# Gate and up of a SwiGLU layer: two of eight pairs of row tiles with seven block products for eight, on one Trainium2 core

## The chip, the cores and the metric

The kernel runs on one core of one Trainium2 chip. The metric is the device time of one execution in microseconds (us). The kernel before takes 2149.98 us, the median of three runs (2149.72 to 2150.53). Engines are named as in the profile: PE (TensorE matmul), PEld (TensorE weight load), DVE (VectorE), ACT (ScalarE), POOL (GpSimd), SP (SyncE, which issues most DMAs).

## What is computed

A decoder trunk of two layers over 256 rows of 2048 columns in float32. Each layer is an attention part and a SwiGLU channel mixer; the change touches only the mixer.

```python
def swiglu(h, w_gate, w_up, w_down):
    return (jax.nn.silu(h @ w_gate) * (h @ w_up)) @ w_down
...
        h = rmsnorm(x, ffn_norm[i])
        x = x + swiglu(h, ffn_w_gate[i], ffn_w_up[i], ffn_w_down[i])
```

`h` is 256 x 2048, `w_gate` and `w_up` are 2048 x 5632, `w_down` is 5632 x 2048. RMSNorm's division is applied after the product (`rstd`), its gains before it.

## The kernel before

**Split products.** A float32 product is made of three fp32r matmuls: high times high, high times low, low times high (`three`, L1490). A "half" is the unit of work of all engines: 128 x 1024 numbers of a weight. ACT rounds them to `w_hi` (`split`, L957), DVE subtracts to get `w_lo` (L1185), and PE uses both in 12 matmuls of 128 x 512 (`half`, L1496). The rows of x, transposed and split, lie ready in `xT_hi` and `xT_lo`, 16 tiles of 128 features by 256 rows.

**Queues and rings.** `walk` (L396) writes one order of work, and each engine walks it and issues its own part, strictly in that order. Weights arrive by SP's DMAs in chunks of 1 MB, two halves each, into the ring `raw` of four. `w_hi` and `w_lo` are rings of four halves (SPLIT = 4). In the place of half n ACT splits half n+3, which waits until PE has finished half n-1; DVE makes the low part of half n+2; PE multiplies half n when its low part is there (`lo_ready`).

**Gate and up.** The 5632 columns are 11 column blocks of 512 (FB = 11). For each, `ff_block` (L580) does a `block` of eight halves for gate into `acc[0:2]`, `gate` (silu by ACT, L1141), a `block` of eight for up into `acc[2:4]`, and `up` (product by DVE into `hid`, L1429). A loop runs it over nine column blocks.

**Hidden values.** They are transposed beside the next gate block, by `hidden` (L570): `hidden_words` (DVE, two copies into 16-bit words, L1441) in the place of half 1, `hidden_turn` (ACT issues four DMA transposes, L1152) in that of half 3, and the copy back into `hT` (DVE, L1451) in that of half 7. `hidden_turn` stands in ACT's own queue, between two splits:

```python
                act.wait_ge(words_ready, n.hT.value(1))
                act.nop(nofuse=True)
                for w in range(2):
                    for m in range(MT):
                        act.dma_start_transpose(wordsT[:, w, :, m * P:(m + 1) * P],
                                                words[:, w, m, :]).then_inc(wordsT_loaded, 16)
```

The down product (`rows`, L596) follows, with the first of its rows beside the last hidden block; its eight sums lie in all eight banks of PSUM (`down_bank`).

Of the kernel before, what the change touches and what calls it, by code (L numbers as in the profile page):

```python
# [22 lines left out]
P = 128  # L23
HD = 64
GROUP = 8
NB = 512
# [7 lines left out]
S384 = 3 * P  # L34

# [33 lines left out]
class Counts:  # L69


    def __init__(self):
        self.half = Count()
        self.chunk = Count()
        self.x = Count()
# [12 lines left out]
    @contextmanager  # L88
    def loop(self, eng, rounds, sets=(0, 0), **per):

        known = {"half": self.half, "chunk": self.chunk, "norm": self.norm, "qkT": self.qkT, "pair": self.pair,
                 "hT": self.hT, "kt": self.kt}
        every = [(v, per.get(k, 0)) for k, v in known.items()] + list(zip(self.sets, sets))
        start = [v.c for v, _ in every]
        with eng.Fori(0, rounds) as i:
            for v, k in every:
                v.i, v.per = (i, k) if k else (None, 0)
            yield i
            for (v, k), c in zip(every, start):
                assert v.c == c + k, (v.c, c, k)  # L100
                v.i, v.c, v.per = None, c + rounds * k, 0
# [87 lines left out]
def decoder_kernel(nc, widths, x_in, attn_norm, ffn_norm, even_w_in, even_q_norm, even_k_norm, even_sinks,  # L189
# [23 lines left out]
    HALVES = 4 + 8 * 8 + 2 * 4 * 8 + 3 * CG * 8 + 2 * (2 * FB * 8 + FK * 2)  # L213
    BQ = AQ + 2 * AK

    with ExitStack() as ctx:
# [13 lines left out]
        x = sb("x", [P, MT, D], F32)  # L230
        with ExitStack() as s1:
# [6 lines left out]
            wordsT = sb("wordsT", [P, 2, 4, SEQ], U16, s1)  # L238
        oT_hi = sb("oT_hi", [P, KT, SEQ], F32R)
# [40 lines left out]
        acc = [ctx.enter_context(nc.psum_tensor(f"acc{i}", [P, NB], F32)) for i in range(4)]  # L280
# [3 lines left out]
        down_bank = [work[0:2], acc[0:2], work[2:4], acc[2:4]]  # L284

        raw_loaded = [sem(f"raw_loaded{i}") for i in range(RAW)]
        first_loaded = sem("first_loaded")
# [66 lines left out]
        def xT_banks(j, pair):  # L354
            return (work[0:2], work[2:4], acc[0:2])[j % 2 if pair is None else pair]
# [36 lines left out]

        TURNS_B = ((19, (31, 32), 35, q_nat, qT, NA // 2), (32, (38, 39), None, k_nat, kT, NA // 2),
                   (41, (53, 54), 55, q_nat, qT, NA // 2 + PAIRS), (49, (56, 57), None, k_nat, kT, NA // 2 + PAIRS))

        def walk(eng, e):  # L396
# [4 lines left out]
            def half(**what):  # L401
                e.half(**what)
                n.half.c += 1
# [57 lines left out]
            def block(acc_set, src=(xT_hi, xT_lo), extra=None, first=False, added=None):  # L461
                x0 = n.xT.c // JB * JB if n.xT.c % JB else n.xT.c - JB
                for k in range(8):
                    half(src=src, kts=(2 * k, 2 * k + 1), acc_set=acc_set, start=k == 0, stop=k == 7,
                         needs=needed(x0, k) if first else None, added=added)
                    if extra:
                        extra(k)
# [78 lines left out]
            def feed_forward(layer):  # L546
# [17 lines left out]
                e.gate(0)  # L564
                n.sets[0].c += 1
                block(1, added=x0)
                e.up(1)
# [12 lines left out]
                def ff_block(j, extra=None):  # L580
                    block(0, extra=lambda k: hidden(j, k))
                    e.gate(0)
                    n.sets[0].c += 1
                    block(1, extra=extra)
                    e.up(1)
                    n.sets[1].c += 1

# [4 lines left out]
                with n.loop(eng, FB - 2, half=16, sets=(1, 1), hT=1) as j:  # L592
                    ff_block(j)
                ff_block(FB - 2, lambda k: stage(0, 0) if k == 5 else None)
# [12 lines left out]
                with n.loop(eng, FK // 4 - 2, half=8, kt=4) as j:  # L607
                    rows(j * 4 + 4)
# [14 lines left out]
                if layer == 0:  # L623
                    xT(1, 1, x0 + 2, pair=0)
                else:
                    down_residual(3)
# [74 lines left out]
            def with_queries(k):  # L701
                if k == 0:
                    down_residual(3, 1)
                if k == 1:
                    xT(1, 2, x0, pair=1)
                if k == 3:
                    xT(1, 3, x0 + 1, pair=0)
                rms(k - 2)
# [18 lines left out]
        class Steps:  # L727


            def __init__(self, begin=nothing, first_tiles=nothing, second_high=nothing, second_turn=nothing, keep_busy=nothing, first_split=nothing, half=nothing, evacuate=nothing,  # L730
# [5 lines left out]
                         x_words=nothing, x_merge=nothing, x_take=nothing):  # L736
# [9 lines left out]
                self.key_merge, self.x_words, self.x_merge, self.x_take = key_merge, x_words, x_merge, x_take  # L746

# [4 lines left out]
        def _(sp):  # L752
            n = Counts()

            def chunk(src, tiles=None):

                if n.chunk.past(RAW):
                    sp.wait_ge(lo_ready, n.chunk.value(1 - RAW, unit=2))
# [5 lines left out]
                n.chunk.c += 1  # L764

# [61 lines left out]
            def feed_forward(layer):  # L827
                columns(w_gate[layer], slice(0, NB), after={1: lambda: turn_x(0), 2: lambda: turn_x(1), 3: lambda: turn_x(2)})
                columns(w_up[layer], slice(0, NB))
                with n.loop(sp, FB - 1, chunk=8) as j:  # L830
                    columns(w_gate[layer], bass.ds(j * NB + NB, NB))
                    columns(w_up[layer], bass.ds(j * NB + NB, NB))
                with n.loop(sp, FK // 4 - 1, chunk=4) as j:
                    for t in range(4):
                        chunk(w_down[layer][bass.ds(j * (4 * P) + t * P, P), :])
# [22 lines left out]
            n.chunk.c += 2  # L858
            for k in range(2, KT // 4):
                load_x(sp, k)  # L860
                columns(even_w_in[0], slice(0, NB), [k])
# [82 lines left out]
        def _(act):  # L944
            def split(more):

                n = e.n
                if n.half.i is None and n.half.c + more >= HALVES:
                    return
                s, r = n.half.slot(SPLIT, more), n.half.slot(2 * RAW, more)  # L950
                if n.half.i is None and n.half.c + more in (0, 2):
                    act.wait_ge(third_loaded if n.half.c + more else first_loaded, 16)
                else:
                    act.wait_ge(raw_loaded[r // 2], n.half.turn(2 * RAW, more, plus=1, unit=16))
                if n.half.i is not None or n.half.c + more >= SPLIT:
                    act.wait_ge(half_used, n.half.value(more + 1 - SPLIT))
                act.activation(w_hi[:, s, :], raw[:, r // 2, (r % 2) * HALF:(r % 2 + 1) * HALF],  # L957
                               ACT.Copy).then_inc(hi_ready, 1)
# [182 lines left out]
            def gate(acc_set):  # L1141
# [5 lines left out]
                for m in range(MT):  # L1147
                    last = act.activation(silu_g[:, m, :], acc[2 * acc_set + m][:, :], ACT.Silu,
                                          scale=rstd[:, m:m + 1])
                last.then_inc(acc_free[acc_set], 1)  # L1150

# [9 lines left out]
            def stage(kt, t):  # L1161
# [3 lines left out]
                if n.kt.past(4):  # L1165
# [5 lines left out]
                      first_split=split, half=lambda **w: split(AHEAD), evacuate=evacuate,  # L1171
# [6 lines left out]
        def _(dve):  # L1178
            def split(more):
                n = e.n  # L1180
                if n.half.i is None and n.half.c + more >= HALVES:
                    return
                s, r = n.half.slot(SPLIT, more), n.half.slot(2 * RAW, more)
                dve.wait_ge(hi_ready, n.half.value(more + 1))
                dve.tensor_tensor(w_lo[:, s, :], raw[:, r // 2, (r % 2) * HALF:(r % 2 + 1) * HALF],  # L1185
                                  w_hi[:, s, :].bitcast(F32), ALU.subtract).then_inc(lo_ready, 1)
# [4 lines left out]
            def first_split(k):  # L1191
                if k < AHEAD - 1:
                    split(k)
# [235 lines left out]
            def up(acc_set):  # L1429
# [5 lines left out]
                for m in range(MT):  # L1435
                    last = dve.scalar_tensor_tensor(out=hid[:, m, :], in0=acc[2 * acc_set + m][:, :],
# [23 lines left out]
            def stage(kt, t):  # L1460
# [5 lines left out]
                      first_split=first_split, half=lambda **w: split(AHEAD - 1), evacuate_kv=evacuate_kv, xT=xT_low,  # L1466
# [8 lines left out]
        def _(pe):  # L1475
# [20 lines left out]
            def half(src=None, kts=None, acc_set=None, start=False, stop=False, width=NB, needs=None,  # L1496
                     added=None, down=None, stage=None, staged_since=0):
                n = e.n
                s = n.half.slot(SPLIT)

                pe.wait_ge(lo_ready, n.half.value(1))
# [16 lines left out]
                else:  # L1518
# [3 lines left out]
                    if start:  # L1522

                        pe.wait_ge(acc_free[down], n.sets[down].value())
# [142 lines left out]
```

## Time and profile before

| | before |
|---|---|
| median of three runs | 2149.98 us |
| span of the profiled execution, first to last instruction | 2147.2 us |
| PE busy | 2141.7 us (100%) |
| DVE busy | 1262.2 us (59%) |
| ACT busy | 1091.3 us (51%) |
| granted TensorE clock | 1.000 |
| DMA, mean | 206 GB/s |

The profile is that of one execution; what lies around its span is the difference to the measured time, here 2.8 us against the median. Matmuls are pipelined: the duration shown for one (389 ns) reaches into the next, so that PE's time for a stretch is read from starts, not from the sum of durations. The "idle before" column of an engine tells how long it sat and who released it.

### The profile page before, as it was taken

The page shows a single profiled execution, that of the slowest core. Times are in us where ns is not written, and L with a number is a line of the kernel's source. Part 1 is how long each engine was busy: PE and PEld are TensorE (multiplying, and loading weights), DVE is VectorE, ACT ScalarE, POOL GpSimd, SP SyncE. Part 2 cuts the span into 40 slices and gives each one's busy share as a digit, 9 for nine tenths or more (in the row PEclk, how much of TensorE's full clock was granted, in tenths as well). Part 3 has the DMA queues.
Part 4 walks back from the last instruction along what each step waited for, and adds up shares of the span by engine and source line. Part 5 has one row for each costly group of instructions (what it writes and reads, how often), then busy time and mean ns, then how long its engine had stood idle before and what let it go on. Part 6 is the DMA issues. An engine that isn't in the chain of part 4 may idle for free.

```text
span 2147.2 us, 27584 instructions
## 1 busy us (share of the span) xinstructions
PE 2141.7 (100%) x9967; PEld 1771.9 (83%) x9967; DVE 1262.2 (59%) x1655; ACT 1091.3 (51%) x1466; POOL 65.6 (3%) x39
## 2 busy tenths in 40 slices
PE   9999999999999999999999999999999999999999
PEld 8888888888888888888888888888888888888887
DVE  6776566555555555555667677775555555555555
ACT  6676656344434444444557576664444444444443
POOL 2101000000000000000011001000000000000000
PEclk9999999999999999999999999999999999999999
DMA  8776456766666665555567777776666666765553
GB/s 279 227 222 213 165 180 206 215 206 205 205 199 210 199 204 204 195 195 188 180 201 239 232 227 244 229 217 205 201 198 210 204 204 202 201 216 190 190 194 136
DMA packets 299284, 442.26 MB, mean 206 GB/s; under 512 B 132080, under 2 KB 134864, under 8 KB 288464
## 3 DMA queue, kind: packets, MB, share of 16 engines
q1 hardware_dynamic: 250928, 429.75, 61.4%
q10 hardware_dynamic: 47968, 11.58, 2.9%
q8 instruction: 43, 0.70, 0.1%
q14 instruction: 25, 0.20, 0.0%
q0 software_dynamic: 320, 0.02, 0.0%
HBM read 408.27 MB, written 2.10 MB: 191 GB/s over the span
## 4 chain that ended last, share of the span: by engine, by line
PE 99%; DVE 1%; ACT 0%; DMA 0%; issue 0%; SPq 0%; ACTq 0%; DVEq 0%
PE acc L1492 28%; PE acc L1494 28%; PE acc L1493 28%; PE work L1494 4%; PE work L1492 4%; PE work L1493 4%; PE work L1590 1%; PE work L1628 1%; PE work L1540 0%; PE work L1601 0%; PE work L1635 0%; DVE w_lo L1185 0%; DMA ident<-in_consts_dram 0%; PE work L1604 0%; ACT p_buf L1124 0%; DVE x L1423 0%
## 5 line engine op out<-in xcount | busy, mean ns | idle before, releaser
L957 ACT ACTIVATE w_hi<-raw 128x1024 fp32r<-128x1024 f32 x756 | 794.4, 1058 | 837.5 <-PE acc L1494 835.5
L1185 DVE TENSOR_TENSOR w_lo<-raw,w_hi 128x1024 fp32r<-128x1024 f32 x756 | 917.3, 1223 | 470.2 <-ACT w_hi L957 469.6
L1492 PE MATMUL acc<-w_hi,xT_hi 128*128 128x512 f32 (+1 forms) x2080 | 809.5, 389 | 0.5 <-DVE w_lo L1185 0.5
L1494 PE MATMUL acc<-w_hi,xT_lo 128*128 128x512 f32 (+1 forms) x2080 | 806.1, 388 | 0.0
L1493 PE MATMUL acc<-w_lo,xT_hi 128*128 128x512 f32 (+1 forms) x2080 | 806.0, 388 | 0.0
L1492 PEld LDWEIGHTS acc<-w_hi,xT_hi 128*128 128x128 f32 x2080 | 390.6, 188 | 84.3 <-DVE w_lo L1185 2.4
L1494 PEld LDWEIGHTS acc<-w_hi,xT_lo 128*128 128x128 f32 x2080 | 390.6, 188 | 80.2
L1493 PEld LDWEIGHTS acc<-w_lo,xT_hi 128*128 128x128 f32 x2080 | 390.7, 188 | 78.9
L1492 PE MATMUL work<-w_hi,stage_hi 128*128 128x512 f32 x352 | 137.0, 389 | 0.0
L1494 PE MATMUL work<-w_hi,stage_lo 128*128 128x512 f32 x352 | 136.9, 389 | 0.0
L1494 PE MATMUL acc<-w_hi,stage_lo 128*128 128x512 f32 x352 | 136.9, 389 | 0.0
L1493 PE MATMUL work<-w_lo,stage_hi 128*128 128x512 f32 x352 | 136.9, 389 | 0.0
L1493 PE MATMUL acc<-w_lo,stage_hi 128*128 128x512 f32 x352 | 136.9, 389 | 0.0
L1492 PE MATMUL acc<-w_hi,stage_hi 128*128 128x512 f32 x352 | 136.9, 389 | 0.0
L1462 DVE TENSOR_TENSOR stage_lo<-hT,stage_hi 128x256 fp32r<-128x256 f32 x88 | 37.4, 425 | 160.9 <-ACT stage_hi L1167 160.9
L1492 PE MATMUL acc<-w_hi,oT_hi 128*128 128x512 f32 x256 | 100.7, 393 | 0.0
L1493 PE MATMUL acc<-w_lo,oT_hi 128*128 128x512 f32 x256 | 99.7, 389 | 0.0
L1494 PE MATMUL acc<-w_hi,oT_lo 128*128 128x512 f32 x256 | 99.7, 389 | 0.0
L1493 PEld LDWEIGHTS acc<-w_lo,stage_hi 128*128 128x128 f32 x352 | 66.1, 188 | 13.7
L1494 PEld LDWEIGHTS work<-w_hi,stage_lo 128*128 128x128 f32 x352 | 66.1, 188 | 13.7
L1494 PEld LDWEIGHTS acc<-w_hi,stage_lo 128*128 128x128 f32 x352 | 66.1, 188 | 13.7
L1493 PEld LDWEIGHTS work<-w_lo,stage_hi 128*128 128x128 f32 x352 | 66.1, 188 | 13.7
(132 smaller groups left out, 1212.0 us busy)
## 6 DMA issues: line engine op xcount, KB each, us to landing
raw<-in_ffn_w_gate_dram SPq DMA_DIRECT2D x88, 1024.0 KB, 5.1
raw<-in_ffn_w_up_dram SPq DMA_DIRECT2D x88, 1024.0 KB, 5.1
raw<-in_ffn_w_down_dram SPq DMA_DIRECT2D x88, 1024.0 KB, 4.7
raw<-in_odd_w_in_dram SPq DMA_DIRECT2D x48, 1024.0 KB, 5.6
raw<-in_even_w_in_dram SPq DMA_DIRECT2D x32, 1024.0 KB, 5.7
raw<-in_even_w_out_dram SPq DMA_DIRECT2D x16, 1024.0 KB, 5.0
raw<-in_odd_w_out_dram SPq DMA_DIRECT2D x16, 1024.0 KB, 6.1
bias<-in_bias_dram SPq DMA_DIRECT2D x24, 384.0 KB, 3.8
```

The lines of the kernel that those rows point to most:

```text
L957: act.activation(w_hi[:, s, :], raw[:, r // 2, (r % 2) * HALF:(r % 2 + 1) * HALF], ACT.Copy).then_inc(hi_ready, 1)
L1185: dve.tensor_tensor(w_lo[:, s, :], raw[:, r // 2, (r % 2) * HALF:(r % 2 + 1) * HALF], w_hi[:, s, :].bitcast(F32), ALU.subtract).then_inc(l ...
L1462: dve.tensor_tensor(stage_lo[:, t, :], hT[:, bass.ds(kt, 1), :].rearrange("p a b -> p (a b)"), stage_hi[:, t, :].bitcast(F32), ALU.subtrac ...
L1492: pe.matmul(out_ps, x_hi, wh, start=start, stop=False)
L1493: pe.matmul(out_ps, x_hi, wl, start=False, stop=False)
L1494: return pe.matmul(out_ps, x_lo, wh, start=False, stop=stop)
L1590: last = pe.matmul(o[rows[b], m, :], v_nat[:, k, h * HD:(h + 1) * HD], pt[:, b, (k + m) * P:(k + m + 1) * P], start=first, stop=stop)
L1628: last = pe.matmul(banks[:, b, lo:hi], qT[rows[b], j % 4, m * P:(m + 1) * P], kT[rows[b], key, 0:hi - lo], start=True, stop=True)
```

## The change

The eight pairs of row tiles (256 rows of the weights each) of a column block are now loaded as pairs: one chunk of `raw` holds gate and up of two row tiles, in two DMAs of 512 KB (`pair_chunk`). Gate and up are computed together into four banks (`work[0:2]` gate, `work[2:4]` up). Six of eight pairs are "eight": two halves of 12 matmuls, as many as before. Two, the pairs 4 and 7 (SEVENS), are "seven": the 2 x 2 block product (two row blocks of x by two row tiles; two row tiles by gate and up) is made as seven products of sums, in four halves of 6, 3, 6 and 6 matmuls. Some of the seven go straight into a `work` bank, four go into banks of their own (`one_g`, `four`, `six`, `five`, the banks of `acc`), which DVE joins in `mix`.

New work around it: sums of the weights by DVE (`make_sums`, once per seven one addition of 128 x 1024 and two of 128 x 512), sums of x per layer (`x_forms`), ACT's copies out of `work` (`direct_out`, four of 128 x 512) and out of `one_g`, and `mix`, whose steps lie in the places of the seven halves after the sevens. Column block 0 is made as before, the last one of eights only; the body for nine column blocks (eight in a loop, one behind) has 20 halves. I number them as steps:

| steps | what | matmuls each | beside them |
|---|---|---|---|
| 0 to 3 | `seven(0)`, pair 4 | 6, 3, 6, 6 | |
| 4 to 7 | pairs 5, 6 | 12 | sums for pair 7 at 4 to 6; `hidden_words` at 6; `hidden_turn` at 7 |
| 8 to 11 | `seven(1)`, pair 7 | 6, 3, 6, 6 | `direct_out` at 9 and 10 |
| 12 to 19 | pairs 0 to 3 of the next column block | 12 | `hidden` at 12, `mix` at 12 to 19, sums for pair 4 at 16 to 18 |

```diff
@@ the order of work
+                def seven(f):
+                    kinds = PARTS["seven"] + AHEAD * ("pair",)
+                    for i in range(len(PARTS["seven"])):
+                        last = f == len(SEVENS) - 1
+                        if last and i == 2:
+                            e.direct_out(1)
+                        half(hi=kinds[i + AHEAD], lo=kinds[i + AHEAD - 1], part=i, f=f, layer=layer)
+                        if last and i in (1, 2):
+                            e.direct_out(2 * i - 2)
...
+                def body(j, more):
+
+                    def middle(i):
+                        if i < 3:
+                            make_sums(i, 1, 1 if i == 0 else 0)
+                        if i == 2:
+                            e.hidden_words()
+                        if i == 3:
+                            e.hidden_turn()
+
+                    def tail(i):
+                        if i == 0:
+                            e.hidden(j)
+                            n.hT.c += 1
+                        if more:
+                            sums_ahead(i)
+                        e.mix(i)
+
+                    seven(0)
+                    eights((5, 6), PARTS["seven"][:AHEAD], middle)
+                    seven(1)
+                    n.direct.c += 1
+                    eights(range(FIRST_K), PARTS["seven"][:AHEAD] if more else AHEAD * ("pair",), tail, held=True)
+                    n.sets[1].c += 2
...
+                with n.loop(eng, FB - 3, half=len(KINDS), made=len(KINDS), raw=16, up=16, sums=2, mix=1, direct=1, sets=(0, 2),
+                            hT=1) as j:
+                    body(j, True)
+                body(FB - 3, False)
...
+                eights(range(FIRST_K, KT // 2), AHEAD * ("plain",), last_chunk, stop=True)
+                e.gate(0, work[0:2])
+                n.sets[0].c += 1
+                e.up(1, work[2:4])
@@ ACT
+                if n.made.past(SPLIT):
+                    act.wait_ge(half_used, n.made.value(1 - SPLIT))
+                out, src = split_views(kind, s, r)
+                act.activation(w_hi[:, s, 0:out], src, ACT.Copy).then_inc(hi_ready, 1)
@@ DVE
+            def mix(i):
...
+                if i == 1:
+                    dve.wait_ge(half_used, n.half.value(-i - 1))
+                    dve.wait_ge(direct_free, n.direct.value(unit=4))
+                    dve.wait_ge(one_out, n.mix.value(1))
+                    dve.tensor_tensor(shared[:, 0, :], shared[:, 0, :], six, ALU.subtract).then_inc(mix_made, 1)
+                    dve.tensor_tensor(silu_g[:, 0, :], one_g, silu_g[:, 0, :], ALU.add).then_inc(mixed, 1)
...
+                if i == 5:
+                    dve.tensor_tensor(hid[:, :, :], acc_all[:, 1:2, :].broadcast_to([P, MT, NB]), hid[:, :, :],
+                                      ALU.add).then_inc(acc_free[1], 1)
@@ PE
+            def seven_part(part, f, layer):
...
+                pe.wait_ge(lo_ready, n.half.value(1))
+                if part == 0:
+                    pe.wait_ge(flo_ready, layer + 1)
+                    three(work[2], *fs[0], wh[0], wl[0], False, last)
+                    done = three(work[0], *xs[0][1], wh[1], wl[1], False, last)
+                if part == 1:
+                    if first:
+                        pe.wait_ge(acc_free[1], n.sets[1].value(-1))
+                    done = three(one_g, *xs[0][0], wh[0], wl[0], first, last)
+                if part == 2:
+                    three(work[1], *xs[1][1], wh[0], wl[0], False, last)
+                    done = three(six, *fs[3], wh[1], wl[1], first, last)
+                if part == 3:
+                    three(four, *fs[1], wh[0], wl[0], first, last)
+                    done = three(five, *fs[2], wh[1], wl[1], first, last)
+                done.then_inc(half_used, 1)
```

`down_bank` now starts with the banks of `acc`, and the first down half on the banks of `work` waits until `up` has read them.

## Rows read from the trace of the kernel before

**Rows 1.** The page: head, part 1 (busy) and the clock line of part 2.
```profile
span 2147.2 us, 27584 instructions
PE 2141.7 (100%) x9967; PEld 1771.9 (83%) x9967; DVE 1262.2 (59%) x1655; ACT 1091.3 (51%) x1466; POOL 65.6 (3%) x39
PEclk9999999999999999999999999999999999999999
```

**Rows 2.** The page, part 4: shares of the chain that ended last, by engine.
```profile
PE 99%; DVE 1%; ACT 0%; DMA 0%; issue 0%; SPq 0%; ACTq 0%; DVEq 0%
```

**Rows 3.** Windows view, 100 us of gate and up: window, busy us (instructions), PEclk, DMA.
```profile
500.00:600.00 100.00, 100.00 (x443) 82.84 (x442) 54.81 (x53) 40.63 (x41) 0.00 (x0) 1.00 0.66 203
```

**Rows 4.** Lines view by form, whole span: form xcount | busy us, mean ns | idle before.
```profile
L1185 DVE TENSOR_TENSOR w_lo<-raw,w_hi 128x1024 fp32r<-128x1024 f32 x756 | 917.3, 1223 | 470.2 <-ACT w_hi L957 469.6
L957 ACT ACTIVATE w_hi<-raw 128x1024 fp32r<-128x1024 f32 x756 | 794.4, 1058 | 837.5 <-PE acc L1494 835.5 <-DMA raw<-in_even_w_in_dram 1.8
L1436 DVE SCALAR_TENSOR_TENSOR hid<-acc,rstd,silu_g 128x512 f32<-128x512 f32 x44 | 31.0, 747 | 70.0 <-PE acc L1494 70.0
L1448 DVE COPY words<-hid 128x1024 uint16<-128x1024 uint16 x44 | 28.3, 686 | 0.0
L1148 ACT ACTIVATE silu_g<-acc,rstd 128x512 f32<-128x512 f32 x44 | 27.8, 683 | 34.5 <-PE acc L1494 34.5
L1456 DVE COPY hT<-wordsT 128x1024 uint16 x36 | 25.0, 751 | 0.0
L1381 DVE TENSOR_TENSOR t_buf<-t_buf,b_keep 128x512 f32<-128x512 f32 x8 | 5.5, 692 | 0.3
```

**Rows 5.** Timeline of ACT, 550 to 562 us: start, us, instruction [idle before].
```profile
550.94 1.06 ACT L957 ACTIVATE w_hi<-raw 128x1024 fp32r<-128x1024 f32 x1 [1.66 <-PE acc L1494]
553.66 1.06 ACT L957 ACTIVATE w_hi<-raw 128x1024 fp32r<-128x1024 f32 x1 [1.66 <-PE acc L1494]
553.79 5.24 ACTq L1158 DMA_TRANSPOSE wordsT<-words  x4
559.15 2.01 ACT L957 ACTIVATE w_hi<-raw 128x1024 fp32r<-128x1024 f32 x2 [4.42 <-PE acc L1494]
561.82 1.06 ACT L957 ACTIVATE w_hi<-raw 128x1024 fp32r<-128x1024 f32 x1 [0.67 <-PE acc L1494]
```

**Rows 6.** Timeline of DVE, the same stretch.
```profile
546.92 2.35 DVE L1185 TENSOR_TENSOR w_lo<-raw,w_hi 128x1024 fp32r<-128x1024 f32 x2
549.19 1.29 DVE L1448 COPY words<-hid 128x1024 uint16<-128x1024 uint16 x2
560.24 2.36 DVE L1185 TENSOR_TENSOR w_lo<-raw,w_hi 128x1024 fp32r<-128x1024 f32 x2 [4.26 <-ACT w_hi L957]
```

**Rows 7.** Timeline, all engines: first matmuls of two halves, four halves apart.
```profile
553.47 0.39 PE L1492 MATMUL acc<-w_hi,xT_hi 128*128 128x512 f32 x1
...
564.35 0.39 PE L1492 MATMUL acc<-w_hi,xT_hi 128*128 128x512 f32 x1
```

**Rows 8.** Tile view of `wordsT`: the transposes, duration ns min/median/max.
```profile
L1158 ACTq DMA_TRANSPOSE wordsT<-words x88: 1206/1299/1665, 379.7 to 1916.4; - x88
DMA to landing us min/median/max: 3.0/4.8/6.9
```

**Rows 9.** Waits view: who waited for whom, us in total, times, longest.
```profile
DVE w_lo L1185 <- ACT w_hi L957: 469.6, 372, 4.4
PEld acc L1492 <- DVE w_lo L1185: 2.4, 5, 0.9
```

**Rows 10.** Timeline, 8.6 to 10.3 us: PE starts when a low part is made.
```profile
8.64 1.23 DVE L1185 TENSOR_TENSOR w_lo<-raw,w_hi 128x1024 fp32r<-128x1024 f32 x1
9.92 0.50 PE L1492 MATMUL acc<-w_hi,xT_hi 128*128 128x512 f32 x1
10.26 0.40 PE L1493 MATMUL acc<-w_lo,xT_hi 128*128 128x512 f32 x1
```

**Rows 11.** The page, part 6: one weight load, KB, us from issue to landing.
```profile
raw<-in_ffn_w_gate_dram SPq DMA_DIRECT2D x88, 1024.0 KB, 5.1
```

More of the change, by code:

```diff
@@ L34, with ends_of_use @@
 S384 = 3 * P
+BODY = ("seven", "eight", "eight", "seven", "eight", "eight", "eight", "eight")
+PARTS = {"seven": ("two", "one", "sums_a", "sums_b"), "eight": ("pair", "pair")}
+KINDS = tuple(kind for of in BODY for kind in PARTS[of])
+FIRST_K = 4
+SEVENS = tuple((FIRST_K + i) % len(BODY) for i, of in enumerate(BODY) if of == "seven")
+def ends_of_use(body):
+    at, out = 0, []
+    for of in body:
+        out.append(at + 2)
+        at += len(PARTS[of])
+    return out, at
 PAIRS = GROUP // 2
@@ L74, in __init__ @@
         self.chunk = Count()
+        self.made = Count()
+        self.raw = Count()
+        self.up = Count()
+        self.sums = Count()
+        self.mix = Count()
+        self.direct = Count()
+        self.ffn = Count()
         self.x = Count()
@@ L563, in feed_forward @@
                 block(0, extra=with_gate, first=True, added=x0 - 1)
-                e.gate(0)
+                e.gate(0, acc[0:2])
                 n.sets[0].c += 1
-                block(1, added=x0)
-                e.up(1)
+                n.ffn.c += 1
+                block(1, extra=e.x_forms, added=x0, then="pair")
+                e.up(1, acc[2:4])
                 n.sets[1].c += 1
@@ L590, in stage, with make_sums, eights @@
                     n.kt.c += 1
-                with n.loop(eng, FB - 2, half=16, sets=(1, 1), hT=1) as j:
-                    ff_block(j)
-                ff_block(FB - 2, lambda k: stage(0, 0) if k == 5 else None)
+                def make_sums(step, f, more):
+                    e.sums(step, f, more)
+                    if step == 2:
+                        n.sums.c += 1
+                def eights(ks, ahead, extra, stop=False, held=False):
+                    kinds = 2 * len(ks) * ("pair",) + ahead
+                    for i in range(2 * len(ks)):
+                        kt = 2 * ks[0] + i
+                        half(hi=kinds[i + AHEAD], lo=kinds[i + AHEAD - 1], kt=kt, start=kt == 0, held=held and kt == 0,
+                             first_sets=kt == 2 and not held, stop=stop and kt == KT - 1, direct_stop=not stop and kt == 2 * SEVENS[-1] - 1)
+                        extra(i)
@@ L735, in __init__ @@
                          nat_merge=nothing, nat_scale=nothing, key_merge=nothing,
-                         x_words=nothing, x_merge=nothing, x_take=nothing):
+                         x_words=nothing, x_merge=nothing, x_take=nothing,
+                         x_forms=nothing, sums=nothing, direct_out=nothing, mix=nothing):
                 self.n, self.begin, self.keep_busy, self.first_split = None, begin, keep_busy, first_split
@@ L746, in __init__ @@
                 self.key_merge, self.x_words, self.x_merge, self.x_take = key_merge, x_words, x_merge, x_take
+                self.x_forms, self.sums, self.direct_out, self.mix = x_forms, sums, direct_out, mix
         block = ctx.enter_context(nc.Block())
@@ L764, in chunk, with pair_chunk @@
                 n.chunk.c += 1
+                n.half.c += 2
+            def pair_chunk(layer, k, cols, halves, freed):
+                sp.wait_ge(lo_ready, n.half.value(-freed))
+                s, u = n.chunk.slot(RAW), n.up.slot(RAW)
+                dst = raw[:, s, :].rearrange("p (t w n) -> p w t n", t=2, w=2)
+                rows = slice(2 * k * P, (2 * k + 2) * P)
+                for w, of, loaded in ((1, w_gate, raw_loaded[s]), (0, w_up, up_loaded[u])):
+                    sp.dma_start(dst[:, w, :, :],
+                                 of[layer][rows, cols].rearrange("(t p) n -> p t n", p=P)).then_inc(loaded, 16)
+                n.chunk.c += 1
+                n.up.c += 1
+                n.half.c += halves
             def columns(w, cols, which=range(KT // 4), after=None):
@@ L944, in _, with split @@
         def _(act):
-            def split(more):
+            def split(kind="plain"):
                 n = e.n
-                if n.half.i is None and n.half.c + more >= HALVES:
+                if n.made.i is None and n.made.c >= HALVES:
                     return
[L950 to L958, printed above, removed]
+                s, r = n.made.slot(SPLIT), n.raw.slot(2 * RAW)
+                if n.made.i is None and n.made.c in (0, 2):
+                    act.wait_ge(third_loaded if n.made.c else first_loaded, 16)
+                elif kind in ("plain", "pair", "two"):
+                    act.wait_ge(raw_loaded[r // 2], n.raw.turn(2 * RAW, plus=1, unit=16))
+                if kind in ("pair", "two"):
+                    act.wait_ge(up_loaded[n.up.slot(2 * RAW) // 2], n.up.turn(2 * RAW, plus=1, unit=16))
+                if kind in ("sums_a", "sums_b"):
+                    act.wait_ge(sums_made, n.sums.value(unit=3))
+                if n.made.past(SPLIT):
+                    act.wait_ge(half_used, n.made.value(1 - SPLIT))
+                out, src = split_views(kind, s, r)
+                act.activation(w_hi[:, s, 0:out], src, ACT.Copy).then_inc(hi_ready, 1)
+                split_over(n, kind)
             def begin():
@@ L1178, in _, with split @@
         def _(dve):
-            def split(more):
+            def split(kind="plain"):
                 n = e.n
-                if n.half.i is None and n.half.c + more >= HALVES:
+                if n.made.i is None and n.made.c >= HALVES:
                     return
[L1183 to L1186, printed above, removed]
+                s, r = n.made.slot(SPLIT), n.raw.slot(2 * RAW)
+                dve.wait_ge(hi_ready, n.made.value(1))
+                out, src = split_views(kind, s, r)
+                dve.tensor_tensor(w_lo[:, s, 0:out], src, w_hi[:, s, 0:out].bitcast(F32), ALU.subtract).then_inc(lo_ready, 1)
+                split_over(n, kind)
@@ L1494, in three @@
                 return pe.matmul(out_ps, x_lo, wh, start=False, stop=stop)
-            def half(src=None, kts=None, acc_set=None, start=False, stop=False, width=NB, needs=None,
-                     added=None, down=None, stage=None, staged_since=0):
+            def seven_part(part, f, layer):
                 n = e.n
                 s = n.half.slot(SPLIT)
+                a, b = 2 * SEVENS[f], 2 * SEVENS[f] + 1
+                xs = [[(xT_hi[:, kt, m * P:(m + 1) * P], xT_lo[:, kt, m * P:(m + 1) * P]) for kt in (a, b)] for m in range(MT)]
+                fs = [(form_hi[:, f, i, :], form_lo[:, f, i, :]) for i in range(4)]
+                wh, wl = ([w[:, s, i * NB:(i + 1) * NB] for i in range(2)] for w in (w_hi, w_lo))
+                first, last = f == 0, f == len(SEVENS) - 1
+                pe.wait_ge(lo_ready, n.half.value(1))
[14 more added lines that the diff above has]
+                done.then_inc(half_used, 1)
@@ new lines, in eight_half @@
+            def eight_half(kt, start, stop, direct_stop, held, first_sets):
+                n = e.n
+                s = n.half.slot(SPLIT)
+                pe.wait_ge(lo_ready, n.half.value(1))
+                if first_sets:
+                    pe.wait_ge(acc_free[1], n.sets[1].value())
+                for w in (1, 0):
+                    wh, wl = (t[:, s, w * NB:(w + 1) * NB] for t in (w_hi, w_lo))
+                    for m in range(MT):
+                        if held and (w, m) != (0, 0):
+                            pe.wait_ge(direct_free, n.direct.value(unit=4) - {(1, 0): 3, (1, 1): 1, (0, 1): 0}[w, m])
+                        rows = slice(m * P, (m + 1) * P)
+                        last = three(work[2 - 2 * w + m], xT_hi[:, kt, rows], xT_lo[:, kt, rows], wh, wl, start,
+                                     stop or direct_stop and (w, m) == (0, 1))
+                last.then_inc(half_used, 1)
@@ new lines, in half @@
+            def half(src=None, kts=None, acc_set=None, start=False, stop=False, width=NB, needs=None,
+                     added=None, down=None, stage=None, staged_since=0, hi=None, lo=None, kt=None, direct_stop=False,
+                     part=None, f=None, layer=None, held=False, first_sets=False):
+                n = e.n
+                s = n.half.slot(SPLIT)
+                if part is not None:
+                    return seven_part(part, f, layer)
+                if kt is not None:
+                    return eight_half(kt, start, stop, direct_stop, held, first_sets)
```

206 lines of the change are left out of this document (171 added, 35 removed).

## The prediction

> **What bounds the kernel now.** I read the page first: PE is busy for 2141.7 of the 2147.2 us, at a granted clock of 1.00 throughout [rows 1], and the chain that ended last is 99% PE [rows 2]. So fewer matmuls are worth their time, as long as PE is fed. The window of 100 us inside gate and up shows PE at 100 us, DVE at 54.8 and ACT at 40.6 [rows 3]: both helpers have room on average. The waits view shows how PE is fed: DVE waits 470 us for ACT's high parts, while the only wait of PE's for a low part that stands there is 2.4 us in five places [rows 9]. The average tells nothing of the tightest place, so I went to the timeline of ACT in one column block [rows 5]. The reader is to see there one odd row among splits that come every 2.72 us (550.94, 553.66): the four transposes of `hidden_turn` hold ACT's queue from 553.79 to 559.03, so that the next split starts at 559.15, 5.49 us after the one before. Then ACT does two in a row.
>
> **Units.** Four halves of 12 matmuls lie between 553.47 and 564.35 [rows 7]: 2.72 us a half, 0.2267 us a matmul. The next timings are DVE's: a low part takes 1.23 us, two in a row start 1.14 apart (546.92 to 549.19) [rows 6]. ACT: 1.06, in a row 0.95 apart [rows 5]. ACT starts its split 0.2 us after PE starts the half that frees the slot (553.47, 553.66) [rows 5, 7]. DVE follows ACT's end by about 0.03 (560.24 after 559.15 + 1.06) [rows 5, 6]. PE follows DVE's end by 0.05 (9.92 after 8.64 + 1.23), and its first matmul then has 0.34 to the next instead of 0.23, so 0.1 for the restart [rows 10].
>
> **What is removed.** Each seven has 21 matmuls for 24. There are 2 in a body, 9 bodies in a layer, 2 layers: 36 x 3 = 108 matmuls, x 0.2267 = 24.5 us. A body takes 186 x 0.2267 = 42.16 us for 43.52. The Trainium skill ("TensorE: Matmul & The Clock Gate", section "Wait — 56ns, not 53.3ns?") gives 215.7 ns from start to start for 512 columns at the full clock; by that the gain would be 23.3 us. The rows here have 226.7 ns, 5% more, and they decide.
>
> **What is added on DVE.** In a body: 18 low parts of 1.22 and 2 of 512 columns at 0.69 = 23.3; sums 2 x (1.22 + 2 x 0.69) = 5.2; `mix` with four of 0.69, two of 1.22 and two of 0.75 = 6.7; words 2 x 0.69 and `hidden` 2 x 0.75 = 2.9 [rows 4]. Sum 38.1 us of 42.2, or about 35 when ops in a row overlap as in [rows 6]: 83 to 90% for about 55% before. The operands in PSUM, the broadcasts and the sums into 2 KB slices have no row of their own; the nearest rows are 0.69 for 512 columns and 1.22 for 1024. I went through the 20 steps with three in-order queues and these durations. PE's start of step 0 is 0, starts of steps: 7 at 12.92, 8 at 15.64, 9 at 17.00, 10 at 17.68, 11 at 19.04. Steps 12 to 19 hold 20 us of DVE's work against 21.8 us of PE's; low parts come 0.6 to 1.8 us ahead of need there, so DVE alone stalls nothing by these rows. Should its ops not overlap at all, the low part of step 2 comes 0.6 us late.
>
> **What is added on ACT.** Two more splits net of their width (18 x 1.06 + 2 x 0.6 = 20.3 for 17), four copies of `direct_out`, one of `one_g` and two silus at 0.68 each [rows 4]: 25 us and the 5.2 of the transposes, of 42.2. `direct_out` waits for PE's parts inside ACT's queue, with the splits of steps 13 to 15 behind it; they come out 0.6 us or more ahead of PE. The `held` waits of step 12 are met: `work[1]` is copied 0.8 us and `work[3]` 0.6 us before their matmuls.
>
> **What is moved, and this carries the forecast.** `hidden_turn` stays behind one split and before another, but the halves after it change. In ACT's queue it now stands in step 7, between the splits of steps 10 and 11. Before, PE had four full halves from the start of the place of the turn to the half whose split comes after it: 10.88 us. Now it has steps 7 to 10: 12 + 6 + 3 + 6 = 27 matmuls = 6.12 us, 4.76 less. The path is: PE starts step 7; +0.20 the split of step 10 starts; +5.49 the split of step 11 starts [rows 5]; +1.06; +0.03 and +1.23 on DVE; +0.05 and +0.10 on PE: 8.16 us. PE waits 8.16 - 6.12 = 2.04 us before step 11, in each of 18 bodies: 36.7 us. In the kernel before the same path has 2.7 to 3.0 us to spare (the low part is there at 561.4, needed at 564.35) [rows 6, 7], which is why it doesn't show. The words must be there when the turn starts: DVE has two low parts, the sums and the words to do in steps 4 to 6, ready 1.2 us before. The transposes land 3.0 to 6.9 us after issue [rows 8], the last one by 24.1 on the clock used above, before ACT's copy of `one_g` (25.6), the first that waits for them. Behind the turn nothing is late again: ACT has 8 us of work to do until step 14 and its lead comes back with the full halves.
> Bounds of the stall: the shortest transpose of 88 took 1.206, the longest 1.665 us [rows 8]. Four of the shortest are 4.82 instead of 5.24, stall 1.62; four of the longest 6.66, stall 3.46. Did the turn wait for the end of the split before it, 0.93 more, 2.97. I take 2.04, since the row is the same queue doing the same four transposes.
>
> **The rest.** Loads: a chunk is asked for some 10 us before its first use, and lands in 5.1 us [rows 11]; halved in size and doubled in number, it costs nothing here. `x_forms` (once a layer, beside the first up block, where DVE has over 1 us free in each half) nothing. At the end of the last column block gate and up now come together: silu 2 x 0.65, product 2 x 0.70, with the links 0.2 + 1.3 + 1.4 + 0.2 = 3.1 us against the 2.72 us of the first down half that doesn't need them: 0.4 us, twice, 0.8 us [rows 4]. There the turn has full halves behind it and costs nothing.
>
> **Sum.** -24.5 + 36.7 + 0.8 = +13.0 us. The profiled span 2147.2 becomes 2160.2, and with the 2.8 us around it that the median of before has, 2163.0 us.
>
> **Rivals.**
> A. The forecast, stall 1.6 to 2.6 us in a body, 2155 to 2174 us: 0.62.
> B. The stall isn't there or is far below 1.3 us: faster. The mechanism is the turn's hold on ACT. Break-even is 24.5 - 0.8 = 23.7 us over 18 bodies, 1.32 us; the four transposes would have to hold ACT for under 4.5 us, 1.13 each. All 88 lie above that [rows 8], which speaks against. If they hid altogether, 2149.98 - 23.7 = 2126 us. It also covers a misreading of mine of where the turn stands. 0.15.
> C. In between, stall about equal to the gain, 2146 to 2154 us: 0.06.
> D. DVE becomes the bound too: its new forms take 15% longer or don't overlap, its 38 us of work chase PE's 42, and the turn waits for late words. With the stall of step 11 at 2.75, 0.64 at step 2 and 0.18 at step 12, a body costs 3.57 - 1.36 = 2.2 us more: +40, 2190 us. For it: 90% load in a strict order; against: the 0.6 to 1.8 us of slack. 0.13.
> E. PE's clock falls in the stalls. If a stall of 2 us made one full half after it run at 1.2 instead of 2.4 GHz, it would take 2.72 us more, 18 x 2.72 = 49 us on top: 2212 us. No row shows a lower clock, the first 6 us with their waits included [rows 1]. 0.04. The Trainium skill (same page, section "HAM oscillation — how this bites in real kernels") has PE fall to the lower clock when idle gaps grow long; no trace so far shows it.
>
> **The range.** 2143 to 2194 us holds A, C, D at its price and the bounds of the stall (2155 to 2189 us by the same sum); outside are B (0.15) and E (0.04). A measurement here tells about 0.2% (4.3 us) from no change. Slower by more: A but for its lowest hundredth, D and E, 0.78; within: C and that hundredth, 0.07; faster: B, 0.15.
>
> **What will show it.** Right: a wait of PE for `w_lo` of about 1.9 to 2.1 us once in each body, 18 times, released by DVE, behind four transposes on ACT; the body's period 44.2 us; 9859 matmuls; DVE at 80% and more in gate and up; clock 1.00. Wrong: no such wait (B); waits of PE at steps 2 or 12 to 14, or DVE without idle time (D); clock below 1.00 (E). If the period is 42.2 us, my reading of the turn fell.

## The result and the profile after

The changed kernel takes 2166.7 us (2165.94 to 2167.55, four runs) against 2150.26 us: 1.0077 of the time before, 95% interval 1.0065 to 1.0089. Slower by 16.4 us, where 13.0 had been forecast (2163.0 us).

| | before | after |
|---|---|---|
| median | 2150.26 us | 2166.7 us |
| span of the profiled execution | 2147.2 us | 2163.8 us |
| PE busy | 2141.7 us | 2125.5 us |
| DVE, ACT busy | 1262.2, 1091.3 us | 1490.3, 1190.5 us |
| DVE in 100 us of gate and up | 54.8 us | 79.5 us |
| start of one body's transposes to the next | 43.52 us (a column block) | 44.2 us |
| mean granted clock | 1.000 | 0.999 |

The page of the kernel after, its head, part 1 and the shares of the chain that ended last, then the waits view (who waited for whom, us in total, times, longest) and the window of gate and up that answers to [rows 3]:

```profile
span 2163.8 us, 28900 instructions
PE 2125.5 (98%) x9859; PEld 1750.9 (81%) x9859; DVE 1490.3 (69%) x1957; ACT 1190.5 (55%) x1630; POOL 65.6 (3%) x39
PE 92%; ACTq 4%; DVE 2%; ACT 1%; issue 0%; DMA 0%; SPq 0%; DVEq 0%
```

```profile
PE acc L1759 <- DVE w_lo L1379: 32.8, 20, 1.9
```

```profile
500.00:600.00 100.00, 94.74 (x416) 77.46 (x415) 79.47 (x86) 56.44 (x67) 0.00 (x0) 1.00 0.60 193
```

PE does 108 matmuls less, is busy for 16 us less, and yet the span is 17 us longer. The chain, which was 99% PE [rows 2], now has ACT's queue with 4% in it, and PE waits 20 times, 32.8 us, for a low part; 18 of these waits, 31.7 us, are one in each body. One body shows where. ACT (the answer to [rows 5]), DVE and PE, start, duration, instruction and idle time before it:

```profile
583.56 1.06 ACT L1115 ACTIVATE w_hi<-sums 128x1024 fp32r<-128x1024 f32 x1 [2.08 <-PE work L1761]
583.69 5.25 ACTq L1350 DMA_TRANSPOSE wordsT<-words  x4
589.05 1.06 ACT L1115 ACTIVATE w_hi<-sums 128x1024 fp32r<-128x1024 f32 x1 [4.43 <-PE acc L1761]
590.02 1.04 ACT L1115 ACTIVATE w_hi<-raw 128x1024 fp32r<-128x1024 f32 x1
```

```profile
581.12 1.28 DVE L1714 COPY words<-hid 128x1024 uint16<-128x1024 uint16 x2
584.66 1.23 DVE L1379 TENSOR_TENSOR w_lo<-sums,w_hi 128x1024 fp32r<-128x1024 f32 x1 [1.65 <-ACT w_hi L1115]
590.14 1.23 DVE L1379 TENSOR_TENSOR w_lo<-sums,w_hi 128x1024 fp32r<-128x1024 f32 x1 [4.26 <-ACT w_hi L1115]
```

```profile
583.37 0.39 PE L1759 MATMUL work<-w_hi,xT_hi 128*128 128x512 f32 x1
...
589.26 0.39 PE L1761 MATMUL acc<-w_hi,form_lo 128*128 128x512 f32 x1
591.42 0.50 PE L1759 MATMUL acc<-w_hi,form_hi 128*128 128x512 f32 x1 [1.78 <-DVE w_lo L1379]
591.76 0.39 PE L1760 MATMUL acc<-w_lo,form_hi 128*128 128x512 f32 x1
```

PE starts step 7 at 583.37. Then come a split, four transposes, and the next split 5.49 us after the last, as before; its low part ends at 591.37, and PE, whose last matmul of step 10 started at 589.26, starts step 11 at 591.42. The words were made at 582.4, 1.3 us before the turn. The profile shows a wait of 1.78 us, counted from the end of a matmul of 0.39 us. Counted from starts it is more: without the wait step 11 would have started 0.23 us after 589.26, at 589.49, so it is 1.93 us late, and 2.04 with the 0.11 us that its first matmul takes beyond the usual 0.23. A wait of 1.72 to 1.88 us stands in every body, at the same place; bodies follow each other after 44.18 to 44.29 us, but for one of 45.89.

That one holds the other finding. PE's timeline behind the wait at 724.11, and windows over it (busy us, PEclk, DMA):

```profile
724.11 0.50 PE L1759 MATMUL acc<-w_hi,form_hi 128*128 128x512 f32 x1 [1.81 <-DVE w_lo L1379]
724.45 0.50 PE L1760 MATMUL acc<-w_lo,form_hi 128*128 128x512 f32 x1
...
725.18 0.63 PE L1759 MATMUL acc<-w_hi,form_hi 128*128 128x512 f32 x1
725.60 0.63 PE L1760 MATMUL acc<-w_lo,form_hi 128*128 128x512 f32 x1
...
728.10 0.39 PE L1760 MATMUL work<-w_lo,xT_hi 128*128 128x512 f32 x1
```

```profile
724.70:728.10 3.40, 3.40 (x9) 2.64 (x8) 2.20 (x3) 3.40 (x6) 0.00 (x0) 0.51 0.00 0
728.10:732.00 3.90, 3.90 (x19) 3.21 (x18) 3.90 (x6) 1.98 (x3) 0.00 (x0) 1.00 0.77 269
```

For 3.4 us the granted clock is at 0.5, that is 1.2 of 2.4 GHz: matmuls start 0.43 us apart instead of 0.23, and the body is 1.7 us longer. The wait ahead of it was 1.81 us; behind three longer ones of this trace (1.83, 1.85 and 1.88 us) the clock stayed. No stretch of the kernel before shows this.

### The profile page after: what moved, and what is told of

Read it like the earlier page. It is cut to its first block, busy times and chain, and to the rows that moved or that the text cites. A ratio compares the mean times of both kernels' runs of the same rounds, so it can differ in the third digit from the quotient of the medians.

```text
span 2163.8 us, 28900 instructions
## 1 busy us (share of the span) xinstructions
PE 2125.5 (98%) x9859; PEld 1750.9 (81%) x9859; DVE 1490.3 (69%) x1957; ACT 1190.5 (55%) x1630; POOL 65.6 (3%) x39
## 4 chain that ended last, share of the span: by engine, by line
PE 92%; ACTq 4%; DVE 2%; ACT 1%; issue 0%; DMA 0%; SPq 0%; DVEq 0%
PE acc L1759 16%; PE acc L1760 15%; PE acc L1761 15%; PE work L1759 14%; PE work L1761 14%; PE work L1760 14%; ACTq L1350 4%; DVE w_lo L1379 1%; PE work L1909 1%; ACT w_hi L1115 1%; PE work L1947 1%; PE work L1859 0%; DMA raw<-in_even_w_in_dram 0%; PE work L1920 0%; PE work L1954 0%
## 5 line engine op out<-in xcount | busy, mean ns | idle before, releaser
L1759 PE MATMUL work<-w_hi,xT_hi 128*128 128x512 f32 x1064 | 414.5, 390 | 0.0
L1761 PE MATMUL work<-w_hi,xT_lo 128*128 128x512 f32 x1064 | 414.2, 389 | 0.0
L1760 PE MATMUL work<-w_lo,xT_hi 128*128 128x512 f32 x1064 | 414.2, 389 | 0.0
L1759 PE MATMUL acc<-w_hi,xT_hi 128*128 128x512 f32 (+1 forms) x836 | 325.6, 389 | 1.1 <-DVE w_lo L1379 1.1
L1761 PE MATMUL acc<-w_hi,xT_lo 128*128 128x512 f32 (+1 forms) x836 | 322.2, 385 | 0.0
L1760 PE MATMUL acc<-w_lo,xT_hi 128*128 128x512 f32 (+1 forms) x836 | 322.1, 385 | 0.0
L1759 PEld LDWEIGHTS work<-w_hi,xT_hi 128*128 128x128 f32 x1064 | 200.0, 188 | 42.0 <-DVE w_lo L1379 0.4
L1759 PEld LDWEIGHTS acc<-w_hi,xT_hi 128*128 128x128 f32 x836 | 157.0, 188 | 36.7 <-DVE w_lo L1379 3.0
L1761 PEld LDWEIGHTS acc<-w_hi,xT_lo 128*128 128x128 f32 x836 | 157.1, 188 | 31.8
L1760 PEld LDWEIGHTS acc<-w_lo,xT_hi 128*128 128x128 f32 x836 | 157.2, 188 | 30.2
```

Source lines behind the costliest of these rows:

```text
L1759: pe.matmul(out_ps, x_hi, wh, start=start, stop=False)
L1760: pe.matmul(out_ps, x_hi, wl, start=False, stop=False)
L1761: return pe.matmul(out_ps, x_lo, wh, start=False, stop=stop)
```

## The experiments

The theory: the four transposes hold ACT's queue for 5.5 us, and with only 6.12 us of PE's work from the start of step 7 to that of step 11, the path of 8.16 us through ACT and DVE sets PE's start. Rival 1: DVE, now busy for 80% of the time and bound to a strict order, is what PE waits for. Rival 2: the fallen clock, or the transposes' own traffic, costs wherever they stand.

| kernel | median | ratio to before [95%] | a body | PE's wait in a body |
|---|---|---|---|---|
| changed | 2166.7 | 1.0077 [1.0065, 1.0089] | 44.2, one 45.9 | 1.72 to 1.88 |
| e1, turn in step 5 | 2127.19 | 0.9894 [0.9878, 0.9911] | 42.16 | none |
| e2, turn in step 6 | 2144.12 | 0.9973 [0.9963, 0.9984] | 42.9 to 43.5 | 0.44 to 1.02 |
| e3, turn in step 8 | 2210.99 | 1.0284 [1.0266, 1.0301] | 45.7 or 47.3 | 3.08 to 3.31 |
| e4, one transpose | 2179.8 | 1.0141 [1.0124, 1.0158] | 42.16, or 44.2 to 46.0 | none or 1.8 to 2.0 |
| e5, before, turn twice (two runs) | 2249.3 | 1.0463 [1.0442, 1.0484] | 47.8 (a block) | 2.27 to 2.82 |
| e7a, e1 and 2 DVE ops | 2127.14 | 0.9894 [0.9878, 0.9911] | 42.16 to 42.22 | none |
| e7b, e1 and 4 DVE ops | 2163.35 | 1.0065 [1.0048, 1.0081] | 44.40 | 0.15 to 0.24, and 1.42 to 1.50 |
| e8, turn on SP | 2126.79 | 0.9893 [0.9876, 0.9909] | 42.16 | none |

**The turn in another step (e1, e2, e3).** The edit of e1; e2 has 1 and 2 for 0 and 1, e3 leaves the words in step 6 and puts the turn behind half 0 of `seven(1)`:

```diff
+                        if i == 0:
+                            e.hidden_words()
                         if i < 3:
                             make_sums(i, 1, 1 if i == 0 else 0)
-                        if i == 2:
-                            e.hidden_words()
-                        if i == 3:
+                        if i == 1:
                             e.hidden_turn()
```

> The changed kernel with the hidden words in step 4 and the four transposes in step 5 instead of steps 6 and 7, nothing else. Theory (the transposes hold ACT for 5.5 us with only short halves behind them): from step 5 to the start of step 9 PE has 42 matmuls, 9.5 us, against a path of 8.16 us, so the wait of PE disappears, a body takes 42.2 us for 44.2, DVE's and ACT's work unchanged; 2150.3 - 24.5 + 0.8 = 2126.6 us, clock 1.000. Rival 1 (DVE at 83 to 90% is what PE waits for): the same work in the same body, so waits stay somewhere, a body stays near 44 us, 2160 us or more. Rival 2 (the fallen clock costs on its own): clock below 1.000 stays.

> As the kernel above with words in step 5, transposes in step 6. Theory: behind them lie steps 6 to 9, 33 matmuls, 7.48 us, against 8.16: PE waits 0.68 us before step 10, a body 42.85 us, 2138.8 us. Rival 1: no difference to the other places. A theory of a fixed cost of the transposes for PE: 44.2 us a body wherever they stand.

> The changed kernel with the transposes one step later, in step 8, words left in step 6. Theory: steps 8 to 11 are 21 matmuls, 4.76 us, against 8.16: PE waits 3.4 us before step 12, a body 45.6 us, 2187.8 us and more if the clock falls in gaps of 3 us. Rival 1: near the 2166.7 us of the changed kernel.

Measured: 2127.19, 2144.12 and 2210.99 us. In e1 the wait is gone, the waits view has only the 2.4 us for a low part that stood there before [rows 9], the body is 42.16 us (42.19 once in each layer), and the clock is 1.000. The same instructions in another order are 39.5 us faster, and DVE is busy for as long as before in the body, 35.6 us against 35.4: the wait is no matter of DVE's load. Page of e1, head and part 1:

```profile
span 2125.0 us, 28900 instructions
PE 2118.6 (100%) x9859; PEld 1751.3 (82%) x9859; DVE 1493.7 (70%) x1957; ACT 1192.7 (56%) x1630; POOL 65.6 (3%) x39
```

e2 came 5.3 us above what was expected. Its transposes hold ACT for 5.19 to 5.78 us, where those of e1 take 5.2 but for the first four, and the bodies follow: 42.90 us with 5.21, 43.26 with 5.54, 43.50 with 5.78. With the shortest holds the body is within 0.05 us of the expected 42.85. Why they vary here isn't shown. The first four of e1 hold ACT for 6.40 us, 1.2 more than the rest, and PE doesn't wait there either: 9.52 us of matmuls against 8.16 leave 1.36. Two of its turns, ACT's timeline:

```profile
576.97 5.21 ACTq L1350 DMA_TRANSPOSE wordsT<-words  x4
582.36 2.01 ACT L1115 ACTIVATE w_hi<-sums 128x1024 fp32r<-128x1024 f32 x2 [4.88 <-PE work L1761]
...
490.51 5.78 ACTq L1350 DMA_TRANSPOSE wordsT<-words  x4
```

e3 came 23 us above. Its bodies are of two kinds, 5 of 45.7 us (expected 45.6) and 13 of 47.3, and windows over the first 3.5 us behind four of its waits show which are which:

```profile
557.30:560.80 3.50, 3.48 (x10) 2.71 (x11) 2.22 (x2) 3.50 (x6) 0.00 (x0) 0.60 0.00 0
604.60:608.10 3.50, 3.48 (x11) 2.72 (x12) 2.22 (x2) 3.50 (x6) 0.00 (x0) 0.67 0.00 0
651.90:655.40 3.50, 3.50 (x15) 2.91 (x16) 2.23 (x2) 3.50 (x6) 0.00 (x0) 1.00 0.02 1
697.60:701.10 3.50, 3.50 (x9) 2.78 (x10) 2.23 (x2) 3.50 (x6) 0.00 (x0) 0.55 0.05 2
```

At 651.9 the clock stays, and that body has 45.7 us. 13 times 1.6 us are 21 of the 23 us that were missing; 18 times the 0.1 by which the other bodies are longer than 45.6 are the rest.

**One transpose for four (e4).** The edit of the issue; the copy back into `hT` becomes four copies of 512 columns.

```diff
-                for w in range(2):
-                    for m in range(MT):
-                        act.dma_start_transpose(wordsT[:, w, :, m * P:(m + 1) * P],
-                                                words[:, w, m, :]).then_inc(wordsT_loaded, 16)
+                act.dma_start_transpose(wordsT[:, :, :, :, :].rearrange("p w m t q -> p (w m t) q"),
+                                        words[:, :, :, :].rearrange("p w m n -> p (w m n)")).then_inc(wordsT_loaded, 16)
```

> The changed kernel with the place kept (step 7), but one DMA transpose of 2048 columns for four of 512; the copy back is four DVE copies of 512 for two of 1024 (0.3 us more of DVE in a body). Theory: ACT is held for about 1.5 instead of 5.2 us, the path is 4.4 us against 6.12, no wait of PE; a body 42.2 us, 2126.6 us. Rival 1: DVE has more to do, so 2167 us or more. If the one transpose holds ACT as long as the four together (cost by columns), 2167 us too.

A miss: 2179.8 us. Tile view of `wordsT` (duration ns min/median/max) and two turns of ACT's timeline:

```profile
L1348 ACTq DMA_TRANSPOSE wordsT<-words x22: 1342/5287/5483, 406.7 to 1930.4; - x22
DMA to landing us min/median/max: 4.0/7.4/22.3
```

```profile
585.03 5.23 ACTq L1348 DMA_TRANSPOSE wordsT<-words  x1
590.39 1.06 ACT L1115 ACTIVATE w_hi<-sums 128x1024 fp32r<-128x1024 f32 x1 [4.42 <-PE acc L1760]
...
629.25 1.34 ACTq L1348 DMA_TRANSPOSE wordsT<-words  x1
```

The one transpose holds ACT as long as the four together in 14 of 18 bodies, and there PE waits as before. In the other four it takes 1.34 us, and exactly these bodies have 42.16 us. So the kernel that was to shorten the hold did it four times, and the wait went with it. The two turns behind the bodies of each layer are short as well, 1.56 to 2.12 us. In the bodies the data lands 7.3 to 7.5 us after issue, whether the hold is short or long. The last turn of each layer lands late, 19.5 and 22.3 us after issue, and there PE has waits of 3.6 and 6.4 us for `stage_lo`. Why the hold is short in 8 of 22 turns stays open.

**The turn on SP's queue (e8).**

```diff
@@ body
-                        if i == 3:
-                            e.hidden_turn()
@@ SP, behind the last pair_chunk of its loop
+                    sp.wait_ge(words_ready, n.hT.value(1))
+                    sp.nop(nofuse=True)
+                    for w in range(2):
+                        for m in range(MT):
+                            sp.dma_start_transpose(wordsT[:, w, :, m * P:(m + 1) * P],
+                                                   words[:, w, m, :]).then_inc(wordsT_loaded, 16)
```

> The changed kernel (words in step 6), with the four transposes of the nine bodies issued by SP, behind the load of pair 3, instead of by ACT; SP's next load is asked for only 12 us later. Theory (what costs is that they stand in ACT's queue before the splits): no wait of PE, a body 42.2 us, 2127 us. If it is the transposes' traffic or the place in time: 2167 us.

2126.79 us. SP's and ACT's timelines of one body:

```profile
575.83 0.42 SPq L902 DMA_DIRECT2D raw<-in_ffn_w_up_dram  x1
576.42 5.17 SPq L985 DMA_TRANSPOSE wordsT<-words  x4
584.93 0.38 SPq L902 DMA_DIRECT2D raw<-in_ffn_w_gate_dram  x1
```

```profile
575.75 1.06 ACT L1121 ACTIVATE w_hi<-sums 128x1024 fp32r<-128x1024 f32 x1 [2.08 <-PE work L1767]
578.47 1.06 ACT L1121 ACTIVATE w_hi<-sums 128x1024 fp32r<-128x1024 f32 x1 [1.66 <-PE work L1767]
579.83 1.06 ACT L1121 ACTIVATE w_hi<-raw 128x1024 fp32r<-128x1024 f32 x1 [0.30 <-PE work L1767]
```

The same transposes, at nearly the same place in time (0.67 us behind the start of ACT's split, where it was 0.13), take 5.17 us on a queue where nothing urgent stands behind them. ACT's next splits come after 2.72 and 1.36 us, the lengths of steps 7 and 8. The transposes' traffic and their place in time are out as causes; ACT's queue is left.

**The path in the kernel before (e5).** The four transposes are issued a second time, into a spare tile.

> The kernel before, with each four transposes issued twice, the second time into a spare tile that nothing reads; nothing else. Theory (path through ACT's queue against the halves behind the turn): ACT is held 5.2 us longer, the path is 13.4 us against 10.88, so PE waits 2.5 us after each of 22 turns: 2150.1 + 55 = 2205 us, more if the clock falls. If what the changed kernel shows belonged to the sums and the products of seven and not to the turn, this kernel would stay at 2150 us.

2249.3 us, without any sum or product of seven. PE waits 2.27 to 2.40 us at 18 of the 22 turns, 2.65 or so counted from starts and with the restart, and 2.8 us at the last but one of each layer. ACT's timeline:

```profile
379.59 1.06 ACT L958 ACTIVATE w_hi<-raw 128x1024 fp32r<-128x1024 f32 x1 [1.66 <-PE acc L1496]
379.71 5.33 ACTq L1160 DMA_TRANSPOSE wordsT<-words  x4
385.07 5.28 ACTq L1160 DMA_TRANSPOSE spare<-words  x4
390.46 2.95 ACT L958 ACTIVATE w_hi<-raw 128x1024 fp32r<-128x1024 f32 x3 [9.82 <-PE acc L1496]
```

The block is 47.8 us for 43.52, so 4.3 and not 2.5 longer: the clock falls at every one of its 22 waits, which costs 1.6 to 1.7 us in a block. The last turn of each layer makes PE wait for `stage_lo`, 4.7 and 5.1 us. 22 x 4.3 = 95 and some 5 more for these two make the 99.6 us.

**How near DVE is (e7a, e7b).** To e1 come two or four additions of 128x1024 in a body whose results nothing reads, in steps 16 and 17, or 15 to 18. Part of the edit of e7a:

```diff
+                if i in (4, 5):
+                    dve.wait_ge(ex_done, n.mix.value(unit=2) + (4, 5).index(i) + 1)
+                    dve.tensor_tensor(hT[:, FK - 4:FK, :].rearrange('p a b -> p (a b)'), x[:, 0, 0:2 * NB], x[:, 1, 0:2 * NB], ALU.add).then_inc(ex_done, 1)
```

> The kernel with words in step 4 and transposes in step 5 (2127.2 us), plus two DVE additions of 128x1024 per body that nothing needs, in steps 16 and 17: 2.3 us more in 42.2, about 37.4 in all. By the three queues step by step, the low part of step 2 comes late: PE waits 0.4 us in a body, 17 loops' worth, 2134 us. By DVE's average share (89%) nothing waits: 2127 us.

> As the one above with four such additions, in steps 15 to 18: 4.6 us more, about 39.6 of 42.2. Step by step: waits of 0.9 and 1.8 us before steps 1 and 2, a body 44.9 us, 2176 us. By the average share (94%): 2127 us.

2127.14 and 2163.35 us: 2.3 us more in a body cost nothing (0.4 a body had been expected), 4.6 us cost 2.24 a body (2.7 expected). DVE's timeline in e7b at the end of a body and the first steps of the next, and PE's there:

```profile
567.57 1.23 DVE L1430 TENSOR_TENSOR hT<-x 128x1024 f32<-128x1024 f32 x1
568.70 1.22 DVE L1448 TENSOR_TENSOR hid<-hid,words 128x1024 f32<-128x1024 f32 x1
569.84 0.69 DVE L1380 TENSOR_TENSOR w_lo<-raw,w_hi 128x512 fp32r<-128x512 f32 x1
570.44 1.42 DVE L1453 SCALAR_TENSOR_TENSOR hid<-hid,rstd,silu_g 128x512 f32<-128x512 f32 x2
571.76 2.36 DVE L1380 TENSOR_TENSOR w_lo<-sums,w_hi 128x1024 fp32r<-128x1024 f32 x2
```

```profile
573.04 0.49 PE L1765 MATMUL work<-w_hi,xT_hi 128*128 128x512 f32 x1 [1.42 <-DVE w_lo L1380]
```

No row of DVE has idle time before it. The low part of step 2 is the first of the last pair, made at 573.0, and PE, whose row stands last, starts step 2 at 573.04 after 1.42 us. So rival 1 is a real limit of this kernel, but it lies more than 2.3 us of DVE's work in a body away from e1, at the place where DVE is fullest. The changed kernel gives DVE the same work in bodies 2.05 us longer; how far its own limit lies no run tells.

## Why the prediction was right

**The gain.** 108 matmuls fewer, 9859 as said; e1 shows them alone: 42.16 us a body, where 42.16 was worked out, and 2127.2 us where gain and ends gave 2126.6. A body is 1.36 us shorter for 6 matmuls, 226.7 ns each. The 215.7 ns of the Trainium skill ("TensorE: Matmul & The Clock Gate", section "Wait — 56ns, not 53.3ns?") don't hold here: the measured spacing is 5% more, and it decides.

**The wait of step 11.** Worked out as 2.04 us with the restart; the bodies have 44.21 against 42.16, 2.05 us. The wait as the profile shows it was forecast at 1.9 to 2.1 us and is 1.72 to 1.88, since the view counts from the end of a matmul that reaches into the next; from starts it is 1.9. Each link of the path has its row above: 583.37 start of step 7, 583.56 split, 589.05 next split, 590.14 low part, 591.42 PE. In e1, e2, the changed kernel and e3, 42, 33, 27 and 21 matmuls lie against the same path, and the wait grows from none to 3.2 us as they get fewer; e8 takes the transposes off ACT's queue and the wait is gone. That puts the cause at ACT's queue and the halves behind it. The margin claimed for the kernel before (2.7 to 3.0 us) is what e5 used up: 5.3 us more hold, 2.65 us of wait.

**No cost on DVE, on SP's queue, in `direct_out` and the held waits.** No wait of PE's stands at step 12 or elsewhere in the bodies. DVE is busy for 76 to 82 us of 100 where 80 and more was said. In a body it is busy for 35.4 us: of the two figures of the prediction, 38.1 and about 35, the one with overlap is right.

**The end of the last column block.** The profile shows 0.23 us of wait, twice; counted from starts and with the restart, PE loses 0.47 us, where 0.4 each was said.

**What failed.** "Clock 1.00". The falling clock (E) had been given 0.04, with a price of 2.72 us in every body; it came in one body of 18, at 1.7 us. The other runs have mean clocks of 0.999 (2166.11 us) and 0.998 (2167.29 and 2167.55 us), and the times go with them. The span's 16.6 us are then: 18 bodies x 0.69 = 12.4, the clock 1.7, the ends 0.9, 0.6 before the first split product (10.49 for 9.92 us [rows 10]; in all eight traces with the change it starts at 10.17 to 10.75, and in e5, made from the kernel before, at 9.92), and 1.0 that I can't place, 0.8 of it in the mixer of layer 0. Against the forecast of 13.0 that is 0.2 more in the bodies, 0.1 more at the ends, and the other three, 3.3, which the sum hadn't.

The time hung on one moved group of instructions, and not on the arithmetic that the change is about: with the turn where 9.5 us of matmuls follow it, the same change makes the kernel 1.1% faster (e1), and beats both.

## What to carry to other kernels

When a change shortens some stages of a tight pipeline, look for what is queued in the helpers' order just ahead of the short stages: a fixed hold there (here the issue of DMA transposes on ACT) needs so much of the bottleneck's work behind it, counted in the new lengths. Issue such DMAs from a queue with nothing urgent behind them, or right ahead of the longest stages. Read slack step by step: with 37.6 us of DVE's work against 42.16 of PE's in a body (89%, e7a) nothing waited, with 39.9 (95%, e7b) PE lost 2.24 us in each, which an average can't tell.

## What the runs showed of the hardware

- Waits of PE of about 2 us can bring its clock down to 1.2 GHz. In the traces it fell at 1 of 18 waits of 1.72 to 1.88 us (after), 3 of 14 of 1.8 to 2.0 us (e4), all 18 of 2.27 to 2.40 us (e5), but only 13 of 18 of 3.08 to 3.31 us (e3), and at none of e2 (up to 1.02 us) and e7b (up to 1.50 us). Each of these falls cost 1.6 to 1.7 us. Other executions of one kernel differ: two of four of the changed kernel have a mean clock of 0.998 for 0.999 and are 1.2 to 1.6 us longer, and two of four of e7b have 0.999 for 1.000, of which no trace was kept. The length of the wait alone doesn't decide it; what else does stays open. The Trainium skill ("TensorE: Matmul & The Clock Gate", section "HAM oscillation — how this bites in real kernels") ties the fall to idle gaps longer than any of the waits counted here; the traces agree that waits bring it, but show it at shorter ones, and not at every longer one.
- DMA transposes of 16-bit words held the queue that issued them for 5.2 us in most cases (5.1 to 6.4) for 2048 columns in four instructions, on ACT as on SP (e8), and for 5.2 to 5.5 us in one instruction (e4), save for eight of 22 cases of 1.34 to 2.12 us.
